# Modulation rows summed by VectorE, an output projection begun early, and a grouped-query stage that starts in the stage before it

## The reference

```python
def hybrid_layer(x, ...):                 # first block, twice
    proj = x @ w_in
    o_dn  = gated_delta_rule_chunked(...) # 4 heads
    o_gla = gla_chunked(...)              # 4 heads
    o = concat(norm(o_dn) * silu(z_dn), norm(o_gla) * silu(z_gla))
    return layer_norm(ALPHA * x + o @ w_out, ln_g, ln_b)

def second_block(x, c, ...):              # two layers
    c_act = silu(c)                       # one row of 1024
    for i in range(2):
        mod = c_act @ ada_w[i] + ada_b[i] # 1024 x 6144: six rows of 1024
        sh1, sc1, g1, sh2, sc2, g2 = split(mod)
        h = x * (1 + sc1) + sh1
        y = neighbourhood_mixer(h) if i == 0 else gqa_mixer(h)
        x = layer_norm(ALPHA * x + (1 + g1) * y)
        h = x * (1 + sc2) + sh2
        x = layer_norm(ALPHA * x + (1 + g2) * moe(h))
```

## Time and profile before

| what | us |
|---|---|
| median of 3 runs | 4958.51 (4958.41 to 4961.59) |
| the profiled execution | 4958.83 |
| its span, first to last instruction | 4957.0 |
| last gated job, layer 1 (674 to 781) | 107 |
| last gated job, layer 2 (1565 to 1672) | 107 |
| output stage 1 (783 to 908) | 125 |
| output stage 2 (1674 to 1802) | 128 |
| combine (3313 to 3368) | 55 |
| grouped-query stage to the first scores (3368 to 3453) | 85 |

### The profile page before, as it was taken

The page is one execution under the profiler, slowest core; times in us unless marked ns, Lnnn a source line. Parts: engine busy times, 40 slices in busy tenths (PEclk is TensorE's granted clock), DMA queues, the critical chain, the costliest instruction groups (busy, mean ns, idle before and its releaser), DMA issues. The chain is left out here.

```text
span 4957.0 us, 54651 instructions
## 1 busy us (share of the span) xinstructions
PE 4563.9 (92%) x22530; PEld 2543.0 (51%) x22530; DVE 1855.9 (37%) x2789; ACT 1141.4 (23%) x1899; POOL 540.9 (11%) x382
## 2 busy tenths in 40 slices
PE   8999999899999889999879999966999997999993
PEld 4555654355565346666444444433666654444441
DVE  4333552433345335445541111122666963111113
ACT  2333121233322112223100000012444510000002
POOL 1221110032211000000000000012221100000001
PEclk9999999999999999999979999987999997999997
DMA  3111053111104511111239999951000025999994
GB/s 98 31 31 30 26 209 113 53 39 31 31 25 160 190 41 25 37 41 55 74 129 350 336 335 336 336 191 28 14 14 35 2 91 210 344 336 335 334 335 152
DMA packets 362693, 691.49 MB, mean 139 GB/s; under 512 B 53659, under 2 KB 139811, under 8 KB 362327
## 3 DMA queue, kind: packets, MB, share of 16 engines
q1 hardware_dynamic: 347143, 632.43, 37.8%
q0 software_dynamic: 14112, 51.39, 2.8%
q10 hardware_dynamic: 1200, 4.24, 0.2%
HBM read 624.20 MB, written 63.82 MB: 139 GB/s over the span
## 5 line engine op out<-in xcount | busy, mean ns | idle before, releaser
L462 PE MATMUL ps<-sb_mixT,sb_work 128*128 128x512 f32 x768 | 359.9, 605 | 9.6 <-ACT sb_x_tok L780 5.5
L2449 DVE TENSOR_TENSOR sb_work<-sb_work,ps 128x512 f32<-128x512 f32 x66 | 45.4, 687 | 862.5 <-PE ps L2368 862.5
L462 PE MATMUL ps<-sb_xT,sb_work 128*128 128x512 f32 x768 | 358.8, 603 | 7.9 <-ACT sb_x_tok L780 5.5
L2368 PE MATMUL ps<-sb_work,sb_xT 128*128 128x512 f32 x800 | 353.5, 595 | 0.8 <-DVE sb_xT L2438 0.8
L2368 PE MATMUL ps<-sb_work,sb_mixT 128*128 128x512 f32 x800 | 353.0, 594 | 0.8 <-DVE sb_mixT L2438 0.8
L1512 PE MATMUL ps<-sb_xT,sb_work 128*128 128x512 f32 x512 | 239.1, 606 | 5.8 <-DMA sb_work<-na_w_qkv 5.8
L2368 PEld LDWEIGHTS ps<-sb_work,sb_xT 128*128 128x128 f32 x800 | 150.2, 191 | 177.9 <-issue 176.7
L2368 PEld LDWEIGHTS ps<-sb_work,sb_mixT 128*128 128x128 f32 x800 | 150.1, 191 | 177.6 <-issue 176.4
L2444 DVE TENSOR_TENSOR sb_work<-ps,sb_work 128x1024 f32<-128x1024 f32 x66 | 80.8, 1225 | 409.9 <-PE ps L2388 409.9
L2418 ACT ACTIVATE sb_work<-ps 128x512 f32<-128x512 f32 x66 | 39.4, 597 | 845.5 <-PE ps L2368 845.5
L2388 PE MATMUL ps<-sb_mixT,sb_work 128*128 128x512 f32 x528 | 232.1, 592 | 0.9 <-ACT sb_work L2430 0.9
(11 more groups left out here) (440 smaller groups left out, 7343.2 us busy)
## 6 DMA issues: line engine op xcount, KB each, us to landing
sb_work<-moe_w_up SPq DMA_DIRECT2D x66, 2048.0 KB, 10.3
sb_work<-moe_w_gate SPq DMA_DIRECT2D x34, 2048.0 KB, 9.9
sb_xT<-moe_w_down SPq DMA_DIRECT2D x33, 2048.0 KB, 10.9
sb_mixT<-moe_w_down SPq DMA_DIRECT2D x33, 2048.0 KB, 10.8
sb_work<-ada_w SPq DMA_DIRECT2D x96, 512.0 KB, 5.9
scratch_y<-sb_work SPq DMA_DIRECT2D x82, 512.0 KB, 10.9
sb_xT<-moe_w_gate SPq DMA_DIRECT2D x16, 2048.0 KB, 10.6
sb_mixT<-moe_w_gate SPq DMA_DIRECT2D x16, 2048.0 KB, 10.7
```

What stands on the lines that cost most here:

```text
L462: last = pe.matmul(m.ps[:, bank, :], b.w[i][:, k, :], m.xT[:, k, half * HALF:(half + 1) * HALF], start=(k == 0), stop=(k == NK - 1))
L2368: last = pe.matmul(m.ps[:, 2 + 2 * (n % 2) + part, :], b.x_turned[n % 2][:, k * P:(k + 1) * P], w[:, k, :], start=(k == 0), stop=(k == NK ...
L2449: dve.tensor_tensor(b.act[n % 2], b.act[n % 2], m.ps[:, 3 + 2 * (n % 2), :], ALU.mult).then_inc(multiplied, 1)
```

## The change

**Modulation.** The sum over the 8 blocks of each row is made on DVE without the sum over the 128 partitions. During the four delta bodies of each layer DVE executes `modulate(j, slot)` at slots 0, 1, 2, 3, 4 and 6: two operations of 128x1024 on `ada_w` blocks that SP loads in pairs. Both blocks of a pair must be taken before SP loads the next pair; after each fourth pair the finished accumulator goes to DRAM, and SP waits for that store. In the last gated job PE reads the six accumulators back with a column of ones: 2 bias matmuls and 2 matmuls a row, 24 in place of 108. A step of filler is one row.

**Output projection.** Behind these rows and 2 empty steps the filler does tiles 1 to 3 of the output projection over the first 6 of their 8 blocks, 36 matmuls of 128x512, one a step, and ACT copies the six partial results to SBUF. Tile 0's 12 matmuls stay in PSUM: 4 stand before the last norm sums and 8 behind them. The output stage takes the tiles in the order 0, 4, 1, 5, 2, 6, 3, 7, and does for tiles 0 to 3 the 4 remaining matmuls; DVE adds the partial result by one operation more a tile (tiles 1 to 3).

**Combine and grouped-query stage.** SP loads group 0's weights in the combine stage. The transposes are copied out after every pair of tiles, in pieces of 128x256, and PE projects tiles 0 to 3 between the transposes into banks 4 to 7. The grouped-query stage projects tiles 4 to 7 into banks 0 to 3 without a wait for evictions, and for group 0 the root, gain and rotation run on DVE. The buffers move so that the combine stage's own don't overlap the weights.

```diff
-MOD_SLOTS = {2: 0, 4: 1, 6: 2, "u": 3, "a5": 4}
+MOD_PAIRS = (0, 1, 2, 3, 4, 6)
+BEGUN_OUT, BEGUN_TILES = 6, 4
+MOD_SLOTS = {1: 3, 2: 5, 4: "part0", 5: "part1", 6: "part2", "u": "part3", "a3": "part4", "a5": "part5"}
...
@@ hybrid_stage, SP
+            def next_pair(pair):
+                sp.wait_ge(ada_taken, 2 * pair + 2)
+                if pair % 4 == 3:
+                    v = pair // 4
+                    sp.dma_start(m.acc_dram[l, v], b.ada_w[1]).then_inc(acc_stored, 16)
+                    sp.wait_ge(acc_stored, 16 * (v + 1))
+                if 2 * pair + 2 < N_MODS * NK:
+                    load_ada(2 * pair + 2)
+                    load_ada(2 * pair + 3)
...
+                pairs_before = (2, 2, 1, 1, 0, 0)
                 if kind == DELTA:
                     for i, name in enumerate(("k1", "q1", "v1", "z1")):
+                        for taken in itertools.islice(pairs, pairs_before[i]):
+                            next_pair(taken)
                         wait_piece(before, name)
                         load_weight(i, delta_column(i, job))
...
-            for n, name in enumerate(("k1", "q1", "zA1", "zB1", "vA1", "vB1")):
+            for v, name in enumerate(("k1", "q1", "zA1", "zB1", "vA1", "vB1")):
                 wait_piece(len(JOBS) - 1, name)
-                load_mod(n)
+                sp.dma_start(b.mod_w[v], m.acc_dram[l, v]).then_inc(w_loaded[v], 16)
             load_out_weights(sp, m, a["w_out"][l], out_loaded)
@@ hybrid_stage, PE: modulation()
+                for v in range(N_MODS):
...
+                    if v < 2:
+                        wait_freed(pe, len(JOBS) - 1, f"vB{v}")
+                    else:
+                        pe.wait_ge(mod_copied, v - 1)
                     for half in range(2):
+                        pe.matmul(outs[half], ident(m, N_MODS)[:, v:v + 1], halves(b.mod_bias)[half],
+                                  start=True, stop=False)
+                    pe.wait_ge(w_loaded[v], 16 * ((len(JOBS) if v < 4 else GLA_HEADS // 2) + 1))
+                    for half in range(2):
+                        last = pe.matmul(outs[half], ones(m)[:, 0:1], halves(b.mod_w[v])[half], start=False, stop=True)
                     last.then_inc(mod_summed, 1)
                     yield
+                for _ in range(2):
+                    yield
+                pe.wait_ge(out_loaded, 16 * (NK // 2))
+                pe.wait_ge(mixed, BEGUN_OUT)
+                for n in range(2 * len(part_of)):
+                    t, half = n // 2 + 1, n % 2
+                    if n < 2:
+                        pe.wait_ge(mod_copied, N_MODS - 1 + n)
+                    else:
+                        pe.wait_ge(part_copied, n - 1)
+                    for k in range(BEGUN_OUT):
+                        last = pe.matmul(m.ps[:, 6 + half, :], m.mixT[:, k, t * P:(t + 1) * P], ...)
...
+                        yield
@@ hybrid_stage, PE: end
+            pe.wait_ge(o_copied, 2 * DN_HEADS + 4 * (GLA_HEADS // 2))
+            begin_output(0, range(4))
             norm_sums(len(JOBS) - 1)
+            begin_output(0, range(4, BEGUN_OUT))
+            begin_output(1, range(BEGUN_OUT))
@@ hybrid_stage, DVE
+            def modulate(j, slot):
+                if slot not in MOD_PAIRS:
+                    return
+                pair = len(MOD_PAIRS) * j + MOD_PAIRS.index(slot)
+                for n in (2 * pair, 2 * pair + 1):
...
+                    dve.wait_ge(ada_loaded[n % 2], 16 * (n // 2 + 1))
...
+                        dve.scalar_tensor_tensor(acc if k < NK - 1 else w, w, c_k, acc, ALU.mult, ALU.add).then_inc(ada_taken, 1)
@@ out_stage
+    order = (0, 4, 1, 5, 2, 6, 3, 7) if begun else range(NT)
...
+                    for k in range(begun if t < BEGUN_TILES else 0, NK):
...
+                if t in part_of:
+                    dve.scalar_tensor_tensor(x, x, ALPHA, part_of[t], ALU.mult, ALU.add).then_inc(part_added, 1)
@@ combine_stage, PE
+            for t in range(3):
+                turn(t)
+            for n in range(GQA_BEGUN):
+                begin_projection(n)
+                turn(3 + n)
+            turn(NT - 1)
@@ grouped_query_stage, DVE
+            for half in range(2):
+                sum_squares(0, half)
+                rotate(dve, st, 0, half)
```

More of the change, by code:

```diff
@@ L10 @@
+import itertools
 import numpy as np
@@ L82 @@
      "pe_done", "act_done", "dve_done", "pool_done", "act_step", "dve_step", "pool_step"]
-    + [f"signal_{n}" for n in range(81)])
+    + [f"signal_{n}" for n in range(87)])
 def end_stage(nc, m):
@@ L853, in modulation @@
                     yield v
+                for n in range(2 * len(part_of)):
+                    act.wait_ge(part_ready, n + 1)
+                    act.copy(halves(part_of[n // 2 + 1])[n % 2], m.ps[:, 6 + n % 2, :]).then_inc(part_copied, 1)
+                    yield f"part{n}"
                 for stored in mod_stored:
@@ L1315, in turn @@
                     last.then_inc(turned, 1)
-            for t in range(NT):
-                if t >= 3:
-                    pe.wait_ge(y_taken, t - 2)
+            for n, t in enumerate(order):
+                if n >= 3:
+                    pe.wait_ge(y_taken, n - 2)
+                first = 0 if t == 0 else begun if t in part_of else 0
                 for half in range(2):
-                    for k in range(NK):
-                        last = pe.matmul(m.ps[:, 2 * (t % 3) + half, :], m.mixT[:, k, t * P:(t + 1) * P],
+                    for k in range(begun if t < BEGUN_TILES else 0, NK):
+                        last = pe.matmul(m.ps[:, 2 * (n % 3) + half, :], m.mixT[:, k, t * P:(t + 1) * P],
                                          m.xT[:, k, half * HALF:(half + 1) * HALF],
-                                         start=(k == 0), stop=(k == NK - 1))
+                                         start=(k == first), stop=(k == NK - 1))
                 last.then_inc(y_ready, 1)
-                if t:
-                    turn(t - 1)
+                if n:
+                    turn(n - 1)
             turn(NT - 1)
@@ L1727, with first_bank, group_buffers, take @@
 GQA_ROOTS = (4, 8)
+GQA_WIDE, GQA_BEGUN = (GROUP + 2) * HD, NT // 2
+def first_bank(piece):
+    return 4 + piece if piece < GQA_BEGUN else piece - GQA_BEGUN if piece < NT else 7
+def group_buffers(m):
+    at, b = [0], Places()
+    def take(n):
+        at[0] += n
+        return m.work[:, at[0] - n:at[0]]
+    half_tiles, n_norm = NT // 2, GROUP + 1
+    b.q = [[take(SEQ) for _ in range(2)] for _ in range(2)]
+    b.k2 = [take(SEQ) for _ in range(2)]
+    b.prob = [[take(SEQ) for _ in range(2)] for _ in range(2)]
+    pieces = [take(HALF) for _ in range(5)] + [m.turned[:, n * HALF:(n + 1) * HALF] for n in range(3)]
+    b.probT = [[pieces[4 * n + 2 * head:4 * n + 2 * head + 2] for head in range(2)] for n in range(2)]
+    b.scratch = take(half_tiles * n_norm * HD)
+    b.square = b.scratch.rearrange("p (t n) -> p t n", t=half_tiles)
+    b.part = [b.scratch[:, n * 320:(n + 1) * 320].rearrange("p (t h d) -> p t h d", t=half_tiles, h=n_norm)
+              for n in range(4)]
+    b.raw = take(NT * GQA_WIDE).rearrange("p (t n) -> p t n", t=NT)
+    b.w = take(NK * GQA_WIDE).rearrange("p (k n) -> p k n", k=NK)
+    return b
+def load_group_weights(sp, weights, w, g, semaphores):
+    for (dst, col, n), semaphore in zip(((slice(0, 4 * HD), g * 4 * HD, 4 * HD),
+                                         (slice(4 * HD, 5 * HD), g * HD + D, HD),
+                                         (slice(5 * HD, 6 * HD), g * HD + (D + KV_HEADS * HD), HD)), semaphores):
+        load_columns(sp, w[:, :, dst], weights, col, n, semaphore)
 def grouped_query_stage(nc, m, a):
@@ L2552, in experts_stage, with combine_stage @@
             end_stage(nc, m)
-def combine_stage(nc, m, l, columns=None, out=None):
+def combine_stage(nc, m, l, columns=None, out=None, first_weights=None):
     s = m.sem
@@ L2613, in weigh, with copy_out @@
                 act.activation(y[t % 4][0], y[t % 4][0], ACT.Copy, scale=m.gates[:, t, 0:1]).then_inc(weighted, 1)
-            def copy_out(half):
-                act.wait_ge(turned, 4 * half + 4)
+            def copy_out(pair):
+                act.wait_ge(turned, 2 * pair + 2)
                 act.wait_ge(columns_ready, 1)
-                for k in range(0, NK, 2):
-                    dst, src = turned_out(k, half)
+                for k in range(NK // 2):
+                    dst, src = turned_out(k, pair)
                     act.activation(dst, src, ACT.Identity, bias=shift[:, k:k + 1],
@@ L2688, in finish, with copy_out @@
                 dve.scalar_tensor_tensor(x, x, m.cols[:, t:t + 1], b_row, ALU.mult, ALU.add).then_inc(x_done, 1)
-            def copy_out(half):
-                dve.wait_ge(turned, 4 * half + 4)
-                for k in range(1, NK, 2):
-                    dst, src = turned_out(k, half)
+            def copy_out(pair):
+                dve.wait_ge(turned, 2 * pair + 2)
```

(2 more changed lines are left out.)

292 lines of the change are left out of this document (156 added, 136 removed).

## The result

The changed kernel takes 4886.6 us (median of four runs, 4882.3 to 4887.5) against 4959.5 us for the kernel before on the same chip: a ratio of 0.985, 95% interval 0.983 to 0.987. The profiled execution took 4887.0 us, its span is 4885.2 us, 71.8 less than before. 4874 was forecast, with 4858 to 4892 as that case's own range.

The account below looks back on a forecast made before the run. PE, busy 92% of the span, was taken to bound the kernel. 4958.8 + 2 (delta bodies) + 1.2 (last gated jobs) - 37 - 22 (output stages) - 29 (combine, grouped-query) = 4874 us; 8-in-10 range 4846 to 4908.

Parts of the forecast that it names:

- that case's own range: Whole kernel: the forecast's main case, 4874 us, chance 0.61, with 4858 to 4892 us as its range.
- the prediction's own signs of being wrong: Wrong if delta bodies grow, the clock row falls under 0.9 in the levels, or the combine stage grows over 16 us.
- slack in the delta bodies: Delta bodies, tightest place at level 3: the subtraction has 3.6 us of slack; +2 us for both layers.
- the levels of the last gated job: Last gated job: PE waits 6.4 us for ACT's row copy; with DVE setting the pace, levels end +5.1 us a layer.
- the terms behind the levels: Last gated job, a layer: less filler in the chunks -4.5 us; four matmuls before the norm sums and eight behind +2.7.
- rival 1: Last gated jobs: each wait drops PE's granted clock, +25 us a layer, 50 in all, 4924 us; chance 0.12.
- Rival 2: Early grouped-query stage gives -14 instead of -29 us, a few us lost elsewhere: about 4892 us; chance 0.14.
- rival 4: Delta bodies: every pair goes ahead of the subtraction and is late, PE waits each level: about 4975 us; chance 0.03.
- rival 3: Last gated job's waits heal, second output stage's cost no clock: 4859 us; with faster rotation and timely gathers 4854; chance 0.10.
- the output stages: Output stages: 48 fewer matmuls each, -41.2 us, less three PE waits: -37 us in the first, -22 in the second.
- combine and grouped-query: Combine stage ends 12 us later, but scores come earlier through begun projections and VectorE's rotation: -29 us, between -36 and -14.

Follow-up runs that it names:

- Run 10: Changed kernel with two more operations of the same size, into an unread buffer, ahead of each of VectorE's 12 modulation operations a delta job: 5008.8 us, ratio 1.010.
- Run 1: Changed kernel with ACT copying modulation rows 0 and 1 ahead of its second exponential in the last gated job: 4865.3 us, ratio 0.980.
- run 2: Changed kernel with the six bias rows of modulation left out and ACT's order kept, so the output lacks the bias: 4863.6 us, ratio 0.980.
- run 7: Changed kernel with ACT copying rows 0 and 1 before its second exponential, rows 2 to 5 before its third, and output transposes two tiles behind: 4835.1 us, ratio 0.975.
- run 6: Changed kernel with ACT copying rows 0 and 1 before its second exponential and rows 2 to 5 before its third, output stages as changed: 4854.1 us, ratio 0.979.
- run 5: Changed kernel with the output stages' transposes and copies of tile n-2, not n-1, behind tile n's products: 4864.1 us, ratio 0.981.
- Run 8: Changed kernel with the first group's rotation moved back from VectorE to GpSimd, begun projections and early weights kept: 4891.0 us, ratio 0.987.
- run 9: Changed kernel with all eight projections in the grouped-query stage, none in the combine stage, early weights and VectorE's rotation kept: 4900.2 us, ratio 0.988.

## Why the prediction was right or wrong

**Right: the bound and the sign; the total with some luck.** The time is 13 us above 4874 and inside the range. That it is not further off is owed to errors of both signs: 25.9 us too little in the last gated jobs, the neighbourhood stage and the small stretches stand against 12.6 too much elsewhere. One of the prediction's own signs of being wrong came true: the clock row in the levels was to stay above 0.9 and is 0.80. The time followed PE's work and waits. The delta bodies are the same to 0.1 us, with twelve more operations of VectorE in each.

**Right: slack in the delta bodies.** 3.6 us was reckoned at the tightest place. Run 10 can check this only roughly: 33.2 us more work a body, less the 10.3 that PE waited for the subtraction, over six places, is 3.8 us a place that was hidden (an estimate; less all of the growth, a mean of 17.2 us with the slow clock in it, it is 2.7). What a pair costs beside GpSimd is to be seen now. VectorE in the second delta job of the changed kernel, and GpSimd beside it:

```profile
250.37 1.28 DVE L1196 SCALAR_TENSOR_TENSOR sb_spare<-sb_v_tok,sb_c_cols,sb_spare 128x1024 f32<-128x1024 f32 x1
...
257.12 2.99 DVE L1196 SCALAR_TENSOR_TENSOR sb_spare<-sb_v_tok,sb_c_cols,sb_spare 128x1024 f32<-128x1024 f32 x1 [1.16 <-DMA sb_v_tok<-ada_w]
260.21 3.19 DVE L1196 SCALAR_TENSOR_TENSOR sb_spare<-sb_mixT,sb_c_cols,sb_spare 128x1024 f32<-128x1024 f32 x1
```

```profile
256.68 2.35 POOL L1078 TENSOR_TENSOR sb_work<-sb_work,sb_const 128x1024 f32<-128x1024 f32 x1
258.98 3.33 POOL L1052 TENSOR_TENSOR sb_x_tok<-sb_x_tok,sb_const 128x1024 f32<-128x1024 f32 x1
```

Alone the operation takes 1.28 us; beside GpSimd's it takes 2.99 and 3.19, a pair 6.2 (the two operations of GpSimd end at 259.03 and 262.31, those of VectorE 1.08 and 1.09 us behind them). GpSimd's second takes 3.33; the same one in the kernel before, with no such operation of VectorE beside it:

```profile
259.29 2.36 POOL L995 TENSOR_TENSOR sb_x_tok<-sb_x_tok,sb_const 128x1024 f32<-128x1024 f32 x1
```

The rule that the two engines lock each other out of a shared port (Trainium skill, SBUF — State Buffer, "SBUF: two separate sides") agrees with these rows; the prediction had priced a pair by it at 5, for one operation of GpSimd; here there are two in a row. The whole fitted into VectorE's idle time here.

**Wrong in size: the levels of the last gated job.** This is the term that failed: "Behind it are rows 2 and 3 (3.6 us, and some 2 us more on a slow clock)". The wait was right (6.4 forecast, 5.95 measured), its place and releaser too. But the 80 records behind it took 20.1 us at 0.50, where four rows of 1.9 us and three halves of 1.09 make 10.9 at full speed: 9.2 us more, not 2, in each layer. The levels grew by 14.2 us and not 5.1, twice. The prediction gives no row for its "2 us"; its nearest is the earlier trace rows, where the clock came back in some 6 us behind a wait of 2.17. Here it took 9 to 20. Run 1 shows that this long stretch goes with the wait; run 2, and the two lengths seen behind the same wait with the same instructions, show that the wait doesn't decide how long it lasts. Together with that, the terms behind the levels came out as forecast: from the first chunk to the output stage -1.9 us, where -4.5 + 2.7 = -1.8 was reckoned.

**Nearer to rival 1 than the forecast said.** Rival 1 had waits drop the clock in every level, 25 us a layer. It did not come as such: over the levels of layer 1 in run 7, with waits of 1.05 to 1.96 us, the clock is 1.00. But one wait of 6 us a layer did over a third of that rival's damage (18.4 of 50 us), and the argument against the rival, that waits up to 1.29 us left the clock alone, holds for the rows that the prediction had and not for runs 1, 6 and 7, where three of six waits of 1.05 us were followed by a fall. The rule that stood beside it (Trainium skill, TensorE: Matmul & The Clock Gate, "HAM oscillation — how this bites in real kernels": bursts parted by waits start cold each time) is told there of waits of about 3 to 5 us, which the prediction left out. It was set against waits of 1.5 us; it should have been applied to the one of 6.4 that the prediction itself had found. By the 0.50 behind it, the trace agrees there.

**The other rivals.** Rival 2 (little from the early stage) and rival 4 (late pairs) did not come. Of rival 3 the part on the early stage did, and gave even more; the waits in the last gated job did not heal, and those of the second output stage cost clock two times of three.

**Right: the output stages.** -39.9 for -39.7, and -27.2 for -24.7. The second is better since the clock fell behind two of its three waits and not all. What was missed is that these waits needn't be: run 5 takes 19.4 us of them away.

**Wrong in size: combine and grouped-query, -37.1 for -29.** The mechanism was right; four parts were costed too high. Counted from the combine stage's first DMA issue (3278.4, before 3313.4) the scores come 36.4 us earlier, 7.6 more than the 28.8 of the prediction's sum. The gathers were to be 3 us late: VectorE's first mixing began 9.6 us behind that issue, against 9.2 before, and PE began its projections 31.7 us behind it, where the prediction's count (3347.5 - 3313.4) had 34.1. The row of four projections and five turns then took 26.8 us for 30.0, its first projection 6.94 and not 8.5. The next four took 22.6 for 24.1. The rotation took 9.1 us a half for 10. Run 8 measures the rotation's gain at 7.8 us (forecast 6.6), run 9 the begun projections' at 17.4.

**Not forecast, and not shown to be the change's: +6.6 us in the neighbourhood stage.** Between 588.5 and 595.5 us were seen in twelve kernels; 595.1 and 589.1 in two that have the same instructions up to its end, and 588.5 and 592.2 in the two with the old ones. The difference lies in the tail, where PE waits 2 to 3 us in each step, and goes with the granted clock there (0.75 and 0.88). Each is read from one profiled execution. What decides between them, these runs don't explain; a comparison of two kernels by whole time alone carries these 7 us, and the 4.3 us of the levels (77.8 or 82.1) too.

## What to carry to other kernels

When work that filled an engine's gaps is replaced, look up in whose order its buffers come free: here one slot of ScalarE's order cost 24 us (run 1, by ratios), where the change as a whole brought 73. A wait of several microseconds on PE is priced with what runs behind it, at the slow level until a row shows the clock back, not with its own length. And where tiles of unlike length alternate, let the dependent step lag by two tiles: the short one doesn't cover the long one's chain.

## What the runs showed of the hardware

PE was granted 0.50 for 20.1 us in which it had no idle time at all, behind a wait of 5.95 us; behind a wait of 7.95 us with the bias rows left out, for 3.6 us. The same instructions behind the same wait had the clock back after 9 to 10 us in four jobs and after 20 in eight. With these rows behind it a wait of 1.05 us was followed by 0.50 for 3 to 7 us in three jobs of six. VectorE's operation on two inputs in SBUF took up to 3.44 us in the delta jobs, where 1.28 is its time alone; met by two operations of GpSimd in a row, it ended 1.1 us behind each.
